# A hybrid decoder step on one core: in the first chunk, 24 GLU and merge tiles move into the attention stage

## The chip, the cores and the metric

The kernel runs on 1 core of one Trainium2 chip. The metric is the device time of one execution in microseconds (us); lower is better. The core has five engines that run side by side and meet at semaphores: TensorE (PE), VectorE (DVE), ScalarE (ACT), GpSimd (POOL) and SyncE (SP), which here only issues transfers. Sixteen DMA engines move the data.

## The reference, cut to what matters

One inference step of one layer over 1024 prompt tokens and 32 sample tokens, all in float32:

```
h = rmsnorm(x);  q, k, v, u, g_att, g_s5 = split(h @ w_in)
att = differential attention(q, k, v)          # 8 heads, causal, two softmaxes per head
s5y = diagonal complex SSM(u)                  # 64 groups x 64 states
z   = gelu(s5y)
s5o = z * sigmoid(z @ w_glu + b_glu)           # the GLU
merged = sigmoid(g_att) * (att @ w_proj_att) + sigmoid(g_s5) * (s5o @ w_proj_s5)
x = x + merged @ w_out
x = x + PEER(rmsnorm(x))                       # 8 heads, 16 gathered expert rows each
y = rmsnorm(x)
```

The GLU needs only z. The S5 half of `merged` needs s5o and h. The attention needs only q, k and v. The attention and the S5 half of `merged` therefore do not depend on each other.

## The kernel before, in words

**Front.** The norm, the projection of u and the whole SSM are computed for all tokens first. z is stored to DRAM; its first 256 columns also stay on chip (`AT_Z0`).

**Chunks and stages.** The rest runs over three chunks of token columns, `CHUNKS = ((0, 2), (2, 5), (5, 9))` in blocks of 128. A chunk passes through stages: `glu`, `s5` (the merge with the S5 gate), `v`, attention, `ga` (the merge with the attention gate), `out`, `query`. Each stage is a block with one in-order program per engine, and all engines meet at its end. The first chunk has 256 columns, and its values are computed earlier, so it has no `v` stage.

**Weight tiles.** GLU, merges, attention projections and queries use 128x1024 weight tiles of 512 KB, streamed through three buffers (`NWB = 3`) in the order of the list `stream`. SP issues the load of tile m once tile m-3 has been used (`load_tile`, L668). `stat_tile` (L674, matmuls on L678) multiplies one tile by the chunk's columns into one PSUM bank and raises `acc_ready`. In the first chunk before the attention there are 8 GLU tiles, 16 merge tiles (per output block a gate tile and a projection tile), and then, in the attention, 16 tiles: K and Q of 8 heads.

**GLU and merge.** For a GLU tile, ACT takes the sigmoid out of PSUM (L1301) and DVE multiplies it with z (L1309). For a merge pair, ACT takes the sigmoid of the gate tile (L1363) and DVE multiplies the projection tile with it (L1373).

**Attention, first chunk.** A unit is one head and one block of 128 queries; there are 8 heads with two units each. Order is written out by hand in `unit(n)` on each engine. Per head PE does: scores of the second unit (L1520, L1523), transposes of the first unit's probabilities (L1543), the K tile of the next head (L678), the value product (L1560), transposes of the second unit, the Q tile of the next head, the value product, K turned by token (L1502), and scores of the next head's first unit. DVE takes row maxima (L1684), forms the probabilities (L1691 to L1697) and copies K out of PSUM (L1672). ACT does the exponentials (L1602), copies probabilities, outputs, Q and K out of PSUM (L1634, L1610, L1587, L1593), and the roots of the per-head norm (L1621). Exponential, square root and sigmoid each need another activation table, and a change of function costs an ACT_TABLE_LOAD.

**Semaphores.** At the start of the first GLU stage SP waits for the last stores of the SSM and clears 60 spent semaphores (L1277), which later stages use again.

**Behind it.** From the first chunk's `query` stage on, POOL gathers expert rows for PEER, and every later stage carries a fixed plan of gather pairs (`PAIR_PLAN`). In the first chunk the plan is empty up to the query stage: `share(0, ...)` returns -2.

Of the kernel before, what the change touches and what calls it, by code (L numbers as in the profile page):

```python
# [56 lines left out]
def hybrid_step(nc, dr, out):  # L57

    root = ExitStack()
    with root:  # L60
        def sem(name):
            return root.enter_context(nc.semaphore(name))
# [1180 lines left out]
        def sem_again(name):  # L1243
# [3 lines left out]
        vslot, ko = lay(5120, [2, TT + 1, P]), lay(7424, [2, 4, P])  # L1247
        kslot, qslot = lay(21504, [2, T]), lay(21504 + 2 * T, [2, 416])
        causal = lay(24448, [P])
        nmax, coef, ssq = lay(24576, [2, 2]), lay(24580, [2, 1]), lay(24584, [2, 3])  # L1250
        junk_a, osb, lsum = lay(24592, [P]), lay(24720, [2, 3, P]), lay(25488, [4, 2])
        rsum = lay(25496, [4, 2])
        qs, ks = lay(25600, [H, NS]), lay(25856, [H, NS])
        names = ("at_in", "ko_ready", "ko_free", "s_ready", "m_ready", "e_ready", "l_ready", "p_ready",
                 "t_ready", "t_free", "o_ready", "o_free", "ss_ready", "rt_ready", "on_ready", "oT_ready", "oT_free",
                 "qs_ready", "part")
        (at_in, ko_ready, ko_free, s_ready, m_ready, e_ready, l_ready, p_ready, t_ready, t_free,
         o_ready, o_free, ss_ready, rt_ready, on_ready, oT_ready, oT_free, qs_ready, part) = (sem_again(n) for n in names)
        hist_in, vh_in, ko_out, k_out = ([sem_again(f"{n}{k}") for k in range(2)] for n in ("hist_in", "vh_in", "ko_out", "k_out"))
        n_units = 0  # L1260

        def stage_glu(c):
            lo, hi = chunk_cols(c)
            W, m0, fa0, gl0 = hi - lo, first_tile(c, "glu"), n_fa, c * KC
            zT = lay(AT_Z if c else AT_Z0, [KC, W])
            s5oT = lay(AT_S5O, [KC, W])
            with nc.Block(no_gpsimd_drain=True) as block:
                @block.sync
                def _(sp):
                    if c == 0:  # L1270
                        sp.wait_ge(sp_out, 16)
                        sp.wait_ge(ss_out, 16)
                        sp.wait_ge(zs_out, 16)
                        for k in range(2):
                            sp.wait_ge(z_out[k], 16 * (KC // 2))
                        for s in to_clear:
                            sp.sem_clear(s)  # L1277
                    for j in range(KC):
                        load_tile(sp, m0 + j + NWB)

                @block.tensor
                def _(pe):
                    if c:
                        pe.wait_ge(hz_in, 16 + 128 * c)
                    for j in range(KC):
                        if j >= 4:
                            pe.wait_ge(fa, fa0 + j - 3)
                        stat_tile(pe, m0 + j, j % 4, zT, W)
                        peer_pe(pe, share(c, "glu", j, KC))

                @block.scalar
                def _(act):
                    for j in range(KC):
                        peer_act(act, share(c, "glu", j, KC), behind=1)
                        if c == 0 and j == 0:
                            for k in range(2):
                                act.wait_ge(z_out[k], 16 * (KC // 2))
# [12 lines left out]

                @block.gpsimd
                def _(pool):
                    peer_pool(pool, share(c, "glu", 0, 1))


        def stage_merge(c, stage, fold):
# [5 lines left out]
            with nc.Block(no_gpsimd_drain=True) as block:  # L1322
                @block.sync
                def _(sp):
                    if not fold:
                        sp.dma_start(causal, dr["causal"]).then_inc(at_in, 16)
# [105 lines left out]
        def stage_attention(c):  # L1432
# [6 lines left out]
            stores = 2 if sampled else 1  # L1439
            N, early = H * nf, nf > 2  # L1440
            def turned(n):

                h = (n - 2) // nf - 1
                return h if (n - 2) % nf == 0 and 0 <= h < H else None
# [8 lines left out]
            with nc.Block(no_gpsimd_drain=True) as block:  # L1453
                @block.sync
                def _(sp):
# [7 lines left out]
                    def k_rows_out(h):  # L1463
# [13 lines left out]
                    for h in range(H):  # L1477
                        for j in (2 * h + 2, 2 * h + 3):
# [10 lines left out]
                def _(pe):  # L1489
                    def k_tile(h):  # L1490
                        if h:
                            pe.wait_ge(ko_free, h0_ + h)
                        stat_tile(pe, m0 + 2 * h, 7, hT, W)

                    def q_tile(h):
                        pe.wait_ge(fv, fv0 + h + 1)
                        stat_tile(pe, m0 + 2 * h + 1, 7, hT, W)

# [34 lines left out]
                    def unit(n):  # L1533
# [50 lines left out]
                def _(act):  # L1584
                    def q_in(h):
                        act.wait_ge(acc_ready, m0 + 2 * h + 2)
                        nc.scalar.activation(qslot[:, h % 2, 0:W], ps[:, 7, 0:W], ACT.Copy, scale=HD ** -0.5).then_inc(fa, 1)  # L1587
# [35 lines left out]
                    def outputs(h):  # L1623
                        act.wait_ge(oT_ready, h0_ + h + 1)
                        nc.scalar.activation(attT[:, h, 0:nf * P], ps[:, 6, 0:nf * P], ACT.Copy, scale=subln[:, 0:1]).then_inc(oT_free, 1)

                    def unit(n):
                        h, i = n // nf, n % nf
# [38 lines left out]
                def _(dve):  # L1667
                    def k_in(h):
                        dve.wait_ge(acc_ready, m0 + 2 * h + 1)
                        if h >= 2 and not sampled:  # L1670
# [34 lines left out]
                    def normalised(h):  # L1705
# [5 lines left out]
                                                ALU.mult).then_inc(on_ready, 1)  # L1711

                    def unit(n):
                        h, i = n // nf, n % nf
# [23 lines left out]
                    for n in range(N):  # L1738
                        unit(n)
                    for n in range(N, N + 3):  # L1740
                        if rooted(n) is not None:
# [487 lines left out]
        for c in range(len(CHUNKS)):  # L2229
            stage_glu(c)  # L2230
            n_fa += KC
            stage_merge(c, "s5", False)
            n_fa, n_fv = n_fa + KC, n_fv + KC
            if c:
                stage_values(c)
            stage_attention(c)
# [118 lines left out]
```

## Time and profile before

| what | value |
|---|---|
| three timed runs | 4268.94, 4269.66, 4274.7 us (median 4269.66) |
| the profiled execution | 4273.91 us, its span 4272.0 us |
| busy share of the span | PE 78%, DVE 70%, ACT 37%, POOL 31% |
| mean granted TensorE clock | 0.923 of full speed |
| gathered rows | 1056 issues of 128 rows, 65.9% of the 16 DMA engines' time |

The shares are means over stages with different limits. The stages that this change touches end at about 578 us of the span; before that POOL has next to nothing to do, and after about 700 us gathers keep the DMA engines busy nine tenths of the time. In the rows below, "idle before" is the time an engine stood still just before an instruction, and the name behind the arrow is what ended it; PEld is the weight load that runs beside the matmuls, and each tile shows as 16 matmuls of 128x256.

### The profile page before, as it was taken

To read this page: it belongs to the slowest core of one execution; us is meant where nothing else is said; L and a number is where in the kernel's file an instruction comes from. 1 tells how busy PE (TensorE), PEld (TensorE's weight loads), DVE (VectorE), ACT (ScalarE), POOL (GpSimd) and SP (SyncE) were. 2 spreads that over 40 slices of the span, in tenths; PEclk is the share of its full clock that TensorE was granted. 3 is DMA by queue.
4 is the path that set the end of the run, shared out by engine and by line. 5 is a ranking of instruction groups with operands and counts; after the bars stand their busy time and mean duration, and the time that the engine had idled before them with its cause. 6 is when DMAs were issued, how large, how long until landed. Compare 5 with 4: busy or idle time off the path is not lost. (4 is left out here: it accounts for less than half of the span.)

```text
span 4272.0 us, 43342 instructions
## 1 busy us (share of the span) xinstructions
PE 3319.6 (78%) x13280; PEld 1895.6 (44%) x13280; DVE 2972.3 (70%) x6144; ACT 1573.3 (37%) x4102; POOL 1305.2 (31%) x1145
## 2 busy tenths in 40 slices
PE   7989888787778688988677587967777777777776
PEld 5757776444544444455566443522222222222221
DVE  6483113788988888899666678976676766666664
ACT  2221321434753243477433233233333333333333
POOL 0100001332223333322332323644444444444443
PEclk9989999899989889989789788999999999999999
DMA  3023346998879999888899988999999999999997
GB/s 136 11 86 127 114 159 219 375 416 327 297 289 403 375 400 396 330 290 289 319 385 397 353 328 344 363 418 419 419 417 409 416 416 414 418 412 399 407 412 314
DMA packets 273722, 1411.58 MB, mean 330 GB/s; under 512 B 39090, under 2 KB 78482, under 8 KB 136402
## 3 DMA queue, kind: packets, MB, share of 16 engines
q0 software_dynamic: 158192, 1126.79, 65.9%
q1 hardware_dynamic: 114914, 281.88, 18.0%
q8 instruction: 106, 1.74, 0.2%
q14 instruction: 126, 1.03, 0.1%
q10 hardware_dynamic: 384, 0.13, 0.0%
HBM read 1367.90 MB, written 38.96 MB: 329 GB/s over the span
## 5 line engine op out<-in xcount | busy, mean ns | idle before, releaser
L953 POOL DMA_INDIRECT arena<-in_uv,arena x1056 | 1243.8, 1178 | 2227.4 <-DVE arena L1063 1328.0
L1053 DVE CUSTOM_DVE_ANT_0 arena<-arena 128x1024 f32<-128x1024 f32 x1056 | 1289.7, 1222 | 531.8 <-DMA arena<-in_uv,arena 504.0
L1193 PE MATMUL ps<-arena 128*128 128x512 f32 (+1 forms) x2288 | 1077.3, 615 | 407.5 <-ACT arena L1160 405.9
L678 PE MATMUL ps<-arena 128*128 128x256 f32 (+2 forms) x3456 | 1097.4, 478 | 125.8 <-DMA arena<-in_w_stat 54.5
L678 PEld LDWEIGHTS ps<-arena 128*128 128x128 f32 x3456 | 675.7, 198 | 510.4 <-issue 337.9
L1193 PEld LDWEIGHTS ps<-arena 128*128 128x128 f32 (+1 forms) x2288 | 410.0, 189 | 1074.1 <-ACT arena L1160 628.7
L1141 ACT ACTIVATE arena<-arena 128x2 f32<-128x2 f32 x528 | 107.2, 203 | 1475.9 <-DVE arena L1053 1444.3
L1063 DVE SCALAR_TENSOR_TENSOR arena<-arena 128x1024 f32<-128x1024 f32 x484 | 618.8, 1279 | 22.6 <-ACT arena L1150 22.5
L1150 ACT ACTIVATE arena<-arena 128x1 f32<-128x1 f32 x1056 | 253.4, 287 | 17.3
L1141 ACT ACT_TABLE_LOAD x168 | 215.5, 1283 | 46.2 <-PEq L1322 29.2
L1160 ACT ACTIVATE arena<-ident,arena 128x128 f32<-128x128 f32 x540 | 187.3, 394 | 8.8
L1862 PE MATMUL ps<-ident,arena 128*128 128x128 f32 x512 | 84.2, 315 | 86.1 <-DMA arena<-in_cache_k 62.4
L2064 PE MATMUL ps<-arena 128*128 128x512 f32 (+1 forms) x288 | 129.0, 609 | 26.8 <-PEq L1322 26.8
L1821 PE MATMUL ps<-arena 128*64 128x128 f32 x1024 | 142.6, 299 | 0.0
L1821 PEld LDWEIGHTS ps<-arena 128*64 128x64 f32 x1024 | 126.6, 152 | 13.0 <-issue 10.5
L307 PE MATMUL ps<-arena 128*128 128x512 f32 (+1 forms) x288 | 127.0, 603 | 3.8 <-PEq L118 3.8
L1684 DVE TENSOR_REDUCE arena<-ps 128x1 f32<-128x384 f32 (+5 forms) x128 | 90.7, 750 | 44.8 <-PE ps L1523 44.8
L959 POOL DMA_DIRECT2D arena<-in_iota x1 | 0.7, 718 | 378.7 <-POOLq L2020 378.7
L1406 PE MATMUL ps<-arena 128*128 128x512 f32 (+1 forms) x224 | 100.7, 612 | 17.7 <-PEq L1322 17.7
L1543 PE MATMUL ps<-ident,arena 128*128 128x128 f32 x288 | 50.1, 308 | 81.8 <-DVE arena L1697 81.7
L1862 PEld LDWEIGHTS ps<-ident,arena 128*128 128x128 f32 x512 | 65.1, 159 | 101.3 <-DMA arena<-in_cache_k 61.3
L1898 ACT ACTIVATE arena<-ps 128x512 f32<-128x512 f32 x128 | 69.5, 590 | 106.1 <-PE ps L1862 101.9
(255 smaller groups left out, 3321.2 us busy)
## 6 DMA issues: line engine op xcount, KB each, us to landing
arena<-in_w_stat SPq DMA_DIRECT2D x216, 512.0 KB
arena<-in_cache_k SPq DMA_DIRECT2D x64, 512.0 KB
arena<-in_cache_v SPq DMA_DIRECT2D x64, 512.0 KB
arena<-in_w_mov SPq DMA_DIRECT2D x14, 2048.0 KB, 12.5
arena<-in_uv,arena POOLq DMA_INDIRECT x1056
arena<-in_x SPq DMA_DIRECT2D x16, 512.0 KB, 9.5
arena<-scr_s POOLq DMA_DIRECT2D x40, 128.0 KB
scr_h<-arena SPq DMA_DIRECT2D x1, 4224.0 KB
```

The costliest lines, as they stand in the source:

```text
L307: last = nc.tensor.matmul(ps[0:rows, n % 4, :], tok, slab[:, k, kc, :], start=(kc == 0), stop=(kc == KC - 1))
L678: last = nc.tensor.matmul(ps[:, bank, 0:w], wbuf[m % NWB][:, kc * P:(kc + 1) * P], moving[:, kc, :], start=(kc == 0), stop=(kc == KC - 1))
L953: pool.indirect_dma_start(ring[s % RING], None, dr["uv"], bass.IndirectOffsetOnAxis(ap=idx[:, g % 4, j:j + 1], axis=0)).then_inc(row_in[s ...
L1053: nc.vector.tensor_tensor_reduce(ring[s % RING][:, 0:D], ring[s % RING][:, 0:D], h2r[:, b % 2, :], 1.0, 0.0, ALU.mult, ALU.add, act_in[:, ...
L1063: nc.vector.scalar_tensor_tensor(accr[:, b % 2, :], ring[s % RING][:, D:2 * D], wgt[:, s % RING:s % RING + 1], accr[:, b % 2, :], ALU.mult ...
L1141: nc.scalar.activation(act_out[:, p % 2, :], act_in[:, k:k + 2], ACT.Gelu).then_inc(gelu_d, 1)
L1150: last = nc.scalar.activation(wgt[:, k + q:k + q + 1], gates[:, g % 4, 2 * r + q:2 * r + q + 1], ACT.Copy, scale=act_out[:, p % 2, q:q + 1])
L1160: nc.scalar.activation(diag[:, n % 4, 0:m], pattern, ACT.Copy, scale=wgt[:, k + q:k + q + 1]).then_inc(diag_d, 1)
L1193: last = nc.tensor.matmul(ps[0:m, 4 * (b % 2) + c, :], diag[:, n % 4, 0:m], ring[s % RING][:, D + 512 * c:D + 512 * (c + 1)], start=start, ...
L1821: last = nc.tensor.matmul(flat_s[:, p * P:(p + 1) * P], qpad[:, h * ROWS:(h + 1) * ROWS], kT[:, n % 2, h, :], start=(h == 0), stop=(h == H ...
L1862: last = nc.tensor.transpose(ps[:, t % 3, j * P:(j + 1) * P], kpg[:, n % NKB, h * P:(h + 1) * P], ident[:, :])
L2064: last = nc.tensor.matmul(ps[0:rows, 2 * (b % 2) + k, :], mT[:, kc, (b - b0) * P:(b - b0) * P + rows], o_slab[:, k, kc, :], start=(kc == 0 ...
```

## The change

The stages `glu` and `s5` of the first chunk are gone as stages. Their 24 tiles ("side tiles", numbered e = 0 to 23: 8 GLU tiles, then 8 pairs of gate and projection) are dealt to the 16 attention units: one before PE's wait for each unit's probabilities and a third at each head's end. The side tiles use PSUM banks 1, 3 and 5. Their sigmoids and products get places in ACT's and DVE's unit order; a projection tile has no sigmoid and a gate tile no product of its own. The weight stream of the chunk is reordered to match. For the first chunk the attention's small buffers move to another part of on-chip memory, the attention gets fresh semaphores, and SP's waits and clears move behind the first head's stores. Chunks 1 and 2 are unchanged.

```diff
+        def first_kq(h, k):
+            return 1 - k if h == 0 else 5 * h - (2 if k else 0)
+        def first_side(e):
+            return 5 * (e // 3) + 2 + (e % 3 if e // 3 == H - 1 else 2 * (e % 3))
+        for h in range(H):
+            for k in range(2):
+                stream[first_kq(h, k)] = T_QK + 2 * h + k
+        for e in range(3 * KC):
+            stream[first_side(e)] = T_GLU + e if e < KC else T_GS + e - KC
...
+        AT_FREE = 27268
+        side_s5, side_g = lay(AT_FREE, [KC, 2 * P]), lay(AT_FREE + 2 * D, [2, 2 * P])
+        AT_SMALL = (AT_FREE + 3 * D, 21504, 21504)
...
@@ stage_attention, SP @@
+                    if c == 0:
+                        sp.dma_start(causal, dr["causal"]).then_inc(at_in, 16)
                     head_in(0)
                     head_in(1)
+                    for m in range(2 if c == 0 else 0):
+                        load_tile(sp, m + NWB)
                     k_rows_out(0)
+                    if c == 0:
+                        sp.wait_ge(sp_out, 16)
...
+                        for s in to_clear:
+                            sp.sem_clear(s)
+                        for h in range(H):
+                            if 0 < h < H - 1:
+                                sp.wait_ge(o_ready, h * nf)
+                                sp.wait_ge(k_out[(h - 1) % 2], 16 * ((h - 1) // 2 + 1))
+                                head_in(h + 1)
+                            for j in range(4 if h < H - 1 else 3):
+                                load_tile(sp, 5 * h + 2 + j + NWB)
+                            if h < H - 1:
+                                k_rows_out(h + 1)
+                                load_tile(sp, 5 * h + 6 + NWB)
@@ stage_attention, PE @@
+                    def side_tile(e):
+                        g, half = side_of(e)
+                        if e >= 3:
+                            old, half_old = side_of(e - 3)
+                            if half_old:
+                                pe.wait_ge(side_merged, old - KC + 1)
+                            else:
+                                pe.wait_ge(side_gate, old + 1)
+                        if half and g == KC:
+                            pe.wait_ge(gl_used, KC)
+                        moving = zT if half is None else side_s5 if half else hT
+                        stat_tile(pe, first_side(e), (1, 3, 5)[e % 3], moving, W)
...
                             scores((n + 1) // nf, (n + 1) % nf)
+                        if c == 0:
+                            side_tile(3 * h + i)
                         pe.wait_ge(p_ready, u + 1)
...
                                 scores(h + 1, 0)
+                        if c == 0 and crossing:
+                            side_tile(3 * h + 2)
...
+                    if c == 0:
+                        pe.wait_ge(hz_in, 16)
                     pe.wait_ge(at_in, 16 * (c + 1))
@@ stage_attention, ACT, unit(n) @@
                             q_in(h + 1)
+                        if c == 0:
+                            for e in (3 * h - 1, 3 * h) if i == 0 else (3 * h + 1,):
+                                if e >= 0:
+                                    side_sigmoid(e)
@@ stage_attention, DVE, unit(n) @@
                             maxima((n + 1) // nf, (n + 1) % nf)
+                        if c == 0 and i == 0 and h:
+                            side_product(3 * h - 2)
+                            side_product(3 * h - 1)
...
+                        if c == 0 and crossing:
+                            side_product(3 * h)
@@ main loop @@
-            stage_glu(c)
-            n_fa += KC
-            stage_merge(c, "s5", False)
             if c:
+                stage_glu(c)
+                n_fa += KC
+                stage_merge(c, "s5", False)
```

What the order of the instructions becomes is shown at three places. First PE in the middle of a head. In the program before, L1520 and L1523 are scores, L1543 and L1530 transposes, L678 with x8 one tile, L1560 the value product and L1502 K by token:

```order
L1523 MATMUL ps<-arena,ident 128x128 x2
L1520 MATMUL ps<-arena 128x256 x2
L1523 MATMUL ps<-arena,ident 128x128 x2
L1543 MATMUL ps<-ident,arena 128x128
L1530 MATMUL ps<-ident,arena 128x128 x2
L678 MATMUL ps<-arena 128x256 x8
L1560 MATMUL ps<-arena 128x128
L1543 MATMUL ps<-ident,arena 128x128 x2
L678 MATMUL ps<-arena 128x256 x8
L1560 MATMUL ps<-arena 128x128 x2
```

In the changed program the same instructions stand on L1571 and L1574 (scores), L1596 and L1581 (transposes), L692 (tiles) and L1613 (value product):

```order
L1574 MATMUL ps<-arena,ident 128x128 x2
L692 MATMUL ps<-arena 128x256 x8
L1571 MATMUL ps<-arena 128x256 x2
L1574 MATMUL ps<-arena,ident 128x128 x2
L692 MATMUL ps<-arena 128x256 x8
L1596 MATMUL ps<-ident,arena 128x128
L1581 MATMUL ps<-ident,arena 128x128 x2
L692 MATMUL ps<-arena 128x256 x8
L1613 MATMUL ps<-arena 128x128
L692 MATMUL ps<-arena 128x256 x8
L1596 MATMUL ps<-ident,arena 128x128 x2
L692 MATMUL ps<-arena 128x256 x8
```

Two of a head's five tiles are the K and Q tiles as before; the other three stand ahead of the second scores, ahead of the first transposes and ahead of the second transposes.

Second ACT from a head's first output copy to the next head's first exponentials. Before, L1610 is the output copy, L1634 the probability copy, L1617 the squares, L1621 the roots, L1587 and L1593 the copies of Q and K, L1602 the exponentials:

```order
L1610 ACTIVATE arena<-ps,arena 128x128
L1634 ACTIVATE arena<-ps 128x256
L1617 ACTIVATE arena<-arena 128x128
L1621 ACT_TABLE_LOAD
L1621 ACTIVATE arena<-arena 128x2
L1587 ACTIVATE arena<-ps 128x256
L1593 ACTIVATE arena<-ps 128x256
L1602 ACT_TABLE_LOAD
L1602 ACTIVATE arena<-ps,arena 128x128 x2
```

In the changed program, with the same operations on L1667, L1704, L1674, L1678, L1644, L1650 and L1659, and a side tile's sigmoid on L1695:

```order
L1667 ACTIVATE arena<-ps,arena 128x128
L1704 ACTIVATE arena<-ps 128x256
L1674 ACTIVATE arena<-arena 128x128
L1678 ACT_TABLE_LOAD
L1678 ACTIVATE arena<-arena 128x2
L1644 ACTIVATE arena<-ps 128x256
L1695 ACT_TABLE_LOAD
L1695 ACTIVATE arena<-ps 128x256
L1650 ACTIVATE arena<-ps 128x256
L1659 ACT_TABLE_LOAD
L1659 ACTIVATE arena<-ps,arena 128x128 x2
```

A sigmoid with a table of its own now stands between the copies of Q and K, ahead of the exponentials.

Third SP at the start. Before, it clears the semaphores (ISA, L1277), loads 8 GLU tiles, the causal mask and 16 merge tiles, and then the attention's values (out_v) and K rows:

```order
L1277 ISA x60
L672 DMA arena<-in_w_stat 128x1024 x8
L1267 UNCONDITIONAL_BRANCH
L1323 UNCONDITIONAL_BRANCH
L1326 DMA arena<-in_causal 128x128
L672 DMA arena<-in_w_stat 128x1024 x16
```

Now:

```order
L1489 DMA arena<-in_causal 128x128
L1475 DMA arena<-out_v 128x2x128 x2
L686 DMA arena<-in_w_stat 128x1024 x2
L1481 DMA out_k<-arena 128x2x128
L1486 DMA scr_k<-arena 128x256
L1504 ISA x60
L686 DMA arena<-in_w_stat 128x1024 x4
L1481 DMA out_k<-arena 128x2x128
```

The mask is now the first transfer of the stage whose first matmul waits for it, and the clears stand behind the first K rows and ahead of the sixth tile's load.

## Rows read from the trace of the kernel before

**Rows 1.** Stretches: busy PE, PEld, DVE, ACT, POOL; then granted clock, DMA share, GB/s

```profile
367.83:398.76 30.93, 29.42 (x128) 25.34 (x129) 3.40 (x8) 5.08 (x9) 0.00 (x0) 0.95 0.47 144
398.76:455.33 56.57, 55.49 (x257) 48.57 (x257) 3.40 (x8) 3.07 (x8) 0.00 (x0) 1.00 0.49 150
455.33:578.03 122.70, 95.43 (x489) 76.31 (x489) 31.00 (x112) 58.15 (x175) 0.00 (x0) 0.94 0.31 99
720.00:4272.00 3552.00, 2693.27 (x9817) 1421.35 (x9815) 2660.66 (x5438) 1393.43 (x3537) 1282.76 (x1125) 0.92 0.94 374
```

**Rows 2.** Timeline of the merge: two gate sigmoids, two tiles apart

```profile
402.49 0.38 ACT L1363 ACTIVATE arena<-ps 128x256 f32<-128x256 f32 x1 [4.73 <-PE ps L678]
409.40 0.38 ACT L1363 ACTIVATE arena<-ps 128x256 f32<-128x256 f32 x1 [6.52 <-PE ps L678]
```

**Rows 3.** Timeline of one head of the attention, all engines

```profile
509.19 0.70 PE L1520 MATMUL ps<-arena 64*128 64x256 f32 x4 [1.53 <-ACT arena L1602]
510.37 0.27 PE L1543 MATMUL ps<-ident,arena 128*128 128x128 f32 x1
510.70 3.62 PE L678 MATMUL ps<-arena 128*128 128x256 f32 x16
514.15 0.39 PE L1560 MATMUL ps<-arena 128*128 128x128 f32 x2
514.36 0.42 DVE L1672 COPY arena<-ps 128x256 f32<-128x256 f32 x1 [3.03 <-PE ps L678]
515.68 0.44 PE L1543 MATMUL ps<-ident,arena 128*128 128x128 f32 x2 [1.14 <-DVE arena L1697]
515.96 3.62 PE L678 MATMUL ps<-arena 128*128 128x256 f32 x16
519.41 0.61 PE L1560 MATMUL ps<-arena 128*128 128x128 f32 x4
519.61 0.38 ACT L1587 ACTIVATE arena<-ps 128x256 f32<-128x256 f32 x1 [1.27 <-PE ps L678]
520.52 0.38 ACT L1593 ACTIVATE arena<-ps 128x256 f32<-128x256 f32 x1 [0.53 <-PE ps L1502]
520.93 1.28 ACT L1602 ACT_TABLE_LOAD   x1
522.22 0.37 ACT L1602 ACTIVATE arena<-ps,arena 128x128 f32<-128x128 f32 x1
523.08 0.70 PE L1520 MATMUL ps<-arena 64*128 64x256 f32 x4 [1.53 <-ACT arena L1602]
```

**Rows 4.** Start of the GLU stage: SP and PE, then one slice as in rows 1

```profile
362.12 0.57 SPq L688 DMA_DIRECT2D arena<-scr_h  x1
364.84 2.54 SPq L715 DMA_DIRECT2D scr_z<-arena  x2
367.83 29.43 PE L678 MATMUL ps<-arena 128*128 128x256 f32 x128 [2.59 <-PEq L698]
...
369.00:370.00 1.00, 1.00 (x4) 0.82 (x3) 0.00 (x0) 0.00 (x0) 0.00 (x0) 0.50 0.55 221
```

**Rows 5.** Line L715, the stores of z

```profile
DMA to landing us min/median/max: 2.6/2.7/4.4
```

**Rows 6.** Groups of ACT, 367 to 578 us: busy us, mean ns, idle before

```profile
L1602 ACT ACT_TABLE_LOAD x7 | 9.0, 1283 | 0.1
L1621 ACT ACT_TABLE_LOAD x7 | 9.0, 1283 | 0.1
L1301 ACT ACTIVATE arena<-ps,b_glu 128x256 f32<-128x256 f32 x8 | 3.8, 474 | 19.5 <-PE ps L678 19.5
```

**Rows 7.** Timeline of PE: the seventh head, and the last one's beginning

```profile
550.86 0.70 PE L1520 MATMUL ps<-arena 64*128 64x256 f32 x4 [1.53 <-ACT arena L1602]
552.82 4.85 PE L678 MATMUL ps<-arena 128*128 128x256 f32 x16
566.44 0.70 PE L1520 MATMUL ps<-arena 64*128 64x256 f32 x4 [1.53 <-ACT arena L1602]
```

More of the change, by code:

```diff
@@ L1247, in hybrid_step, with att_small @@
         vslot, ko = lay(5120, [2, TT + 1, P]), lay(7424, [2, 4, P])
[L1248 to L1252, printed above, removed]
+        def att_small(at):
+            return (lay(at, [2, T]), lay(at + 2 * T, [2, 416]), lay(at + 2944, [P]), lay(at + 3072, [2, 2]), lay(at + 3076, [2, 1]),
+                    lay(at + 3080, [2, 3]), lay(at + 3088, [P]), lay(at + 3216, [2, 3, P]), lay(at + 3984, [4, 2]), lay(at + 3992, [4, 2]))
+        AT_FREE = 27268
+        side_s5, side_g = lay(AT_FREE, [KC, 2 * P]), lay(AT_FREE + 2 * D, [2, 2 * P])
+        AT_SMALL = (AT_FREE + 3 * D, 21504, 21504)
         qs, ks = lay(25600, [H, NS]), lay(25856, [H, NS])
+        kslot, qslot = att_small(AT_SMALL[-1])[0:2]
         names = ("at_in", "ko_ready", "ko_free", "s_ready", "m_ready", "e_ready", "l_ready", "p_ready",
@@ L1257, in hybrid_step @@
         (at_in, ko_ready, ko_free, s_ready, m_ready, e_ready, l_ready, p_ready, t_ready, t_free,
-         o_ready, o_free, ss_ready, rt_ready, on_ready, oT_ready, oT_free, qs_ready, part) = (sem_again(n) for n in names)
-        hist_in, vh_in, ko_out, k_out = ([sem_again(f"{n}{k}") for k in range(2)] for n in ("hist_in", "vh_in", "ko_out", "k_out"))
+         o_ready, o_free, ss_ready, rt_ready, on_ready, oT_ready, oT_free, qs_ready, part) = (sem(n) for n in names)
+        side_gate, side_merged = sem("side_gate"), sem("side_merged")
+        hist_in, vh_in, ko_out, k_out = ([sem(f"{n}{k}") for k in range(2)] for n in ("hist_in", "vh_in", "ko_out", "k_out"))
         n_units = 0
@@ L1269, in _ @@
                 def _(sp):
[L1270 to L1277, printed above, removed]
                     for j in range(KC):
@@ L1294, in _ @@
                         peer_act(act, share(c, "glu", j, KC), behind=1)
-                        if c == 0 and j == 0:
-                            for k in range(2):
-                                act.wait_ge(z_out[k], 16 * (KC // 2))
                         act.wait_ge(acc_ready, m0 + j + 1)
@@ L1440, in stage_attention, with kq_tile, side_of @@
             N, early = H * nf, nf > 2
+            kslot, qslot, causal, nmax, coef, ssq, junk_a, osb, lsum, rsum = att_small(AT_SMALL[c])
+            zT, mT = lay(AT_Z0, [KC, W]), lay(AT_MT, [KC, W])
+            def kq_tile(h, k):
+                return m0 + 2 * h + 1 - k if c else first_kq(h, k)
+            def side_of(e):
+                return (e, None) if e < KC else (KC + (e - KC) // 2, (e - KC) % 2)
             def turned(n):
@@ L1475, in _ @@
                     head_in(1)
+                    for m in range(2 if c == 0 else 0):
+                        load_tile(sp, m + NWB)
                     k_rows_out(0)
-                    for h in range(H):
+                    if c == 0:
+                        sp.wait_ge(sp_out, 16)
+                        sp.wait_ge(ss_out, 16)
+                        sp.wait_ge(zs_out, 16)
+                        for k in range(2):
+                            sp.wait_ge(z_out[k], 16 * (KC // 2))
+                        for s in to_clear:
[10 more added lines that the diff above has]
+                                load_tile(sp, 5 * h + 6 + NWB)
+                    for h in range(H if c else 0):
                         for j in (2 * h + 2, 2 * h + 3):
@@ L1625, in outputs, with side_sigmoid @@
                         nc.scalar.activation(attT[:, h, 0:nf * P], ps[:, 6, 0:nf * P], ACT.Copy, scale=subln[:, 0:1]).then_inc(oT_free, 1)
+                    def side_sigmoid(e):
+                        g, half = side_of(e)
+                        if half:
+                            return
+                        act.wait_ge(acc_ready, first_side(e) + 1)
+                        if g >= 2:
+                            if g - 2 < KC:
+                                act.wait_ge(gl_used, g - 1)
+                            else:
+                                act.wait_ge(side_merged, g - 1 - KC)
+                        bias = {} if e >= KC else {"bias": b_glu[:, e:e + 1]}
+                        nc.scalar.activation(side_g[:, g % 2, :], ps[:, (1, 3, 5)[e % 3], 0:W], ACT.Sigmoid, **bias).then_inc(side_gate, 1)
                     def unit(n):
@@ L1711, in normalised, with side_product @@
                                                 ALU.mult).then_inc(on_ready, 1)
+                    def side_product(e):
+                        g, half = side_of(e)
+                        if half == 0:
+                            return
+                        dve.wait_ge(side_gate, g + 1)
+                        if half is None:
+                            nc.vector.tensor_tensor(side_s5[:, g, :], zT[:, g, :], side_g[:, g % 2, :], ALU.mult).then_inc(gl_used, 1)
+                        else:
+                            dve.wait_ge(acc_ready, first_side(e) + 1)
+                            nc.vector.tensor_tensor(mT[:, g - KC, :], ps[:, (1, 3, 5)[e % 3], 0:W], side_g[:, g % 2, :],
+                                                    ALU.mult).then_inc(side_merged, 1)
                     def unit(n):
@@ L1739, in _ @@
                         unit(n)
+                    for e in (3 * H - 2, 3 * H - 1) if c == 0 else ():
+                        side_product(e)
                     for n in range(N, N + 3):
```

17 lines of the change are left out of this document (8 added, 9 removed).

## The prediction

> **What bounds the kernel now.** I read the stretches by stage first [rows 1]. In the GLU and merge stages PE is busy 29.42 of 30.93 us and 55.49 of 56.57 us: PE alone sets their length, and ACT and DVE work about 3 to 5 us in each. In the attention stage PE is busy only 95.43 of 122.70 us, so about 27 us of it are waits, and ACT works 58.15 us there. None of the three stages carries gathers. Everything behind them, the gathers with their DMA share of 0.94 included, starts when they have ended, so what they lose or gain should move the end by the same amount.
>
> Then I read the timeline of one head [rows 3]. PE's second scores start at 509.19 and the next head's at 523.08: 13.89 us per head. PE stands still twice. It waits 1.53 us before the second scores, because ACT must copy Q and K, load the exponential table and do the first exponentials (519.61 to about 523.0) before the score banks are free. It waits 1.14 us before the second transposes, because DVE's K copy (514.36), queued ahead of the probabilities, waits for the K tile. Both are latencies of a chain, not a lack of throughput.
>
> **The change part by part.** All sums are made against the profiled execution: 4273.91 us, span 4272.0.
>
> *Removed:* the two stages, 367.83 to 455.33 [rows 1]: -87.5 us, with their launch gaps and the GLU's slow first tiles.
>
> *Added to PE:* 24 tiles. Two tiles lie 6.91 us apart in the merge (402.49 to 409.40, [rows 2]), so a tile costs 3.455 us and 24 cost +82.9.
>
> *The waits the tiles cover.* I walk one middle head with T = 0 at its second scores, with the steps of [rows 3]: scores until 1.18, side tile A until 4.64, transposes, K tile 4.97 to 8.42, value product 0.39, side tile B until 12.27, second transposes 0.28, Q tile until 16.00, then value product, K by token and first scores (13.89 - 1.53 - 10.22 = 2.14) until 18.14, side tile C until 21.60, next second scores. Without a wait that is 13.89 + 10.37 - 2.67 = 21.59. A tile shows 3.62 but the next instruction starts 3.45 later; this overlap of 0.17 now also holds at the two places where a wait stood, so I take 21.25: 3.0 saved per head (2.67 at least). From head 0's second scores to head 7's there are seven such steps: -21.0 (bounds -18.7 and -21.0).
>
> *Are the chains now in time?* First the exponentials. Q's copy starts 0.20 after its tile; before, the second scores could go 3.67 after the tile's end (519.41 to 523.08). The new sigmoid between the copies costs a table load of 1.28 and 0.47 [rows 6], of which 0.53 fills ACT's idle time before the K copy (520.52, [rows 3]): release at 3.67 + 1.75 - 0.53 = 4.9. PE arrives at 2.14 + 3.46 = 5.6, or 5.3 with the overlap. It fits by 0.4 to 0.7 us: the tightest place. Second the probabilities. ACT's whole attention work is 58.15 / 8 = 7.3 us per head [rows 1], of which about 2.2 are table loads [rows 6]; the half after the first transposes is some 2.5 to 3. So its sigmoids end at about 4.64 + 3 + 1.28 + 0.95 = 9.9. DVE then does a product and the K copy (0.42 each; the product has its shape) and needs 0.9 more (515.68 - 514.78): 11.6, against PE's arrival at 12.27. It fits by 0.6. Per head ACT gets to about 10.5 of 21 us: the 7.3, 14 more loads (14 x 1.28 / 8 = 2.2) and 16 sigmoids (0.9).
>
> *Weight loads.* A merge tile's load is issued when the tile three before it is done, which leaves two tiles, 6.9 us, and PE does not wait for it in the merge [rows 1]. In the new order K and score work lies between, so the lead is 7.7 us or more, and I cost the loads at nothing. This needs SP on time: it now stands in front of them with K row stores, which wait for ACT's K copy, with value loads, and once with the 60 clears. The clears run while head 0's chain and tile 2 hold PE; without that cover they would be late once by a few us.
>
> *The last head.* It has no K and Q tiles. Before it takes 566.44 to 578.03, 11.59 us [rows 1, 7]. The tiles there cover the probability wait and some of ACT's work behind the last value product, but one more root table load (1.28) comes on the path, because sigmoids now stand between the roots. I take -2.4 (bounds 0 and -4).
>
> *The start.* The attention's first matmul now waits for the mask, whose load SP can issue only at the stage's start, about 367.9, behind the z stores (364.84 and after); DMA is still at 221 GB/s at 369 to 370 [rows 4]. No row shows the mask alone. Stores of z take 2.6 to 4.4 us to land, 2.7 in the median [rows 5]. Before, PE started at 367.83. So +2.7; from below 0, since hT's load (362.12) is early enough, from above 4.6.
>
> *TensorE's clock.* The GLU's first tiles ran at a granted clock of 0.50, the 1.2 GHz level, after PE had stood 2.59 us [rows 4], and that slowness went with the removed stage: 29.43 us against 8 x 3.455 = 27.6. The first K tile now starts after a longer stop: +1.6 (0 to 3.5, a whole tile at half rate). In the seventh head the tile at 552.82 took 4.85 and the head 566.44 - 550.86 = 15.58 [rows 7], 1.7 more than usual, after the 1.53 wait. With PE closed up I take that as gone: -1.7 (0 to -1.7).
>
> *One new wait.* The first projection tile (e = 9) needs all 8 GLU products. The last stands on DVE behind the row maxima of the second scores, while PE is at the tile right after these scores. Maxima of a size like the K copy's, twice, and a product of 0.42 give +1.5 once (0 to 2.2).
>
> Sum: -87.5 + 82.9 - 21.0 - 2.4 + 2.7 + 1.6 - 1.7 + 1.5 = -23.9. That is 4250.0 for the profiled execution. The median of the runs shown, 4269.66, is 4.25 below that execution, so I forecast 4246 us.
>
> **A rule that speaks against the change.** In the trace a change of function costs ACT 1.28 us and nothing around it: the load at 520.93 starts 0.03 after the K copy's end and the exponential starts at 522.22, right behind it [rows 3]. Now there are 29 loads (8 exponential, 8 root, 13 sigmoid, counted in the program) for 15 before. The Trainium skill, page "ScalarE: Activation LUTs", section "What ACT_TABLE_LOAD costs", puts a switch at about 1283 ns plus a drain of about 1380 ns, 2.66 us, and its section on table sets asks to batch calls by set. By its drain the two switches in front of the exponentials would cost 2.8 us more and PE would wait some 2 us at each of five head ends, some 10 us in all. The trace shows the load's length as the page has it, and no drain.
>
> **The rivals.**
>
> *ACT's switches bind.* If a switch costs twice its row, 1.28 more, the exponentials are released at 4.9 + 2.56 = 7.5 against PE's 5.6: 1.9 us of new wait at the five head ends that have a sigmoid there (h = 0, 1, 2, 3, 5), +9.6: 4256. For it: the margin there is only 0.4 to 0.7. Against it: no gap in [rows 3]. The page named above states such a price.
>
> *Given back behind 720 us.* The later stages hold 2693 us of PE work at a granted clock of 0.92 [rows 1]. A clock lower by 0.005 would cost at most 0.005 x 2693 / 0.92 = 15 us: 4246 + 15 = 4261. Nothing in these stages changes but their start, so the sign is open; the three runs lie 5.8 us apart.
>
> *Slower: the loads' queue closes a ring.* SP's load of the next head's tile B stands behind the K row stores, which wait for ACT's K copy, which now stands behind a sigmoid, which waits for PE. In the walk the K copy ends at 16.0 + 0.20 + 0.38 + 1.75 + 0.38 = 18.7, the load is released by PE at 21.6, and its tile is used 8.8 us later, 1.9 more than the 6.9 that do in the merge. PE waits once ACT is later than 2.9 + 1.9 = 4.8 us. The gain is gone when each of seven heads loses 3.4 us, with ACT 8.2 late, and at 11 us late the kernel is 7 x 6.2 - 23.9 = 19.5 slower: 4289. Only several long stops on ACT per head could do this; it is half busy.
>
> *The tiles cover nothing.* If the chains simply shift behind the tiles, only launch gaps and start terms are left: -87.5 + 82.9 + 2.7 + 1.6 + 1.5 = +1.2, 4271, no change. Against it: both waits start before the tile's place in PE's order, not behind it.
>
> **How the numbers follow.** Forecast 0.80, with its own terms at their bounds from 4238 to 4257; ACT's switches 0.06; given back 0.06; tiles cover nothing 0.03; the ring 0.05. A measurement of this kernel can tell about 0.2%, 8.5 us, from no change. Faster by more, below 4261: the forecast, the switches and half of what is given back, 0.88. Within 0.2%: 0.07. Slower: 0.05. The range of 8 in 10 runs from 4238, the lower bounds together, to 4261.
>
> **What would show it.** Right: a stage from about 368 to 553 in place of 367.83 to 578.03, 21.3 us from second scores to second scores, PE busy over 93% in it, no wait before second scores and second transposes. Start: the first tile at 370 to 371. The new wait: one stop of about 1.5 us ahead of tile 9 in the fourth head. Wrong: heads above 23 us with PE released by the exponentials (switches) or by in_w_stat (ring), or a stage that is short as said while the stretch behind it is longer than 3694 us, the 4272.0 - 578.0 of before.

## The result, and the profile after

In the first comparison the kernel after took 4238.25 us (median of 4 runs, 4232.8 to 4251.76), the kernel before 4272.18 (4 runs, 4268.94 to 4275.98): a ratio of 0.9929, with a 95% interval of 0.9909 to 0.9949. Timed again (e1, 5 runs), it took 4247.22 against 4270.76: 0.9951, 0.9939 to 0.9964. The two intervals overlap from 0.9939 to 0.9949, some 22 to 26 us. The forecast was 4246, a gain of 23.9, with a range of 4238 to 4261. The first median stands at the very lower end of that range, the second next to the forecast.

The profiled execution of after took 4251.76 us, span 4250.0, the longest of its four. Its stage in the form of [rows 1] (span of the stretch, busy PE, PEld, DVE, ACT, POOL, then granted clock, DMA share, GB/s), and what lies behind it:

```profile
372.54:563.04 190.50, 175.41 (x873) 146.90 (x873) 38.37 (x131) 83.17 (x206) 0.00 (x0) 0.97 0.44 137
...
563.04:4250.00 3686.96, 2823.03 (x10352) 1519.89 (x10352) 2686.70 (x5503) 1407.89 (x3566) 1289.26 (x1137) 0.92 0.93 368
```

One stage of 190.50 us stands where three stood, counted from the end of the last turn of z (PE's last transposes of z, with which the front ends). In before that end is at 365.24 and the next stage starts at 578.03: 212.79. So the stage gave 22.3 us. The span is 22.0 shorter, but not by the stage alone: the front, whose code is the same, ended 7.3 us later (372.54 for 365.24), and the stretch behind the stage was 7.0 shorter (3686.96 for 3693.97). These two are taken up under e1 and e8.

One head in the steady stretch, PE and then ACT, beside [rows 3] (start, duration, engine, line, operation; the bracket is idle time and its releaser):

```profile
501.33 0.70 PE L1571 MATMUL ps<-arena 64*128 64x256 f32 x4
...
502.51 3.62 PE L692 MATMUL ps<-arena 128*128 128x256 f32 x16
...
509.97 3.62 PE L692 MATMUL ps<-arena 128*128 128x256 f32 x16
513.43 0.38 PE L1596 MATMUL ps<-ident,arena 128*128 128x128 f32 x2
513.65 3.62 PE L692 MATMUL ps<-arena 128*128 128x256 f32 x16
517.10 0.61 PE L1613 MATMUL ps<-arena 128*128 128x128 f32 x4
...
519.08 3.62 PE L692 MATMUL ps<-arena 128*128 128x256 f32 x16
522.63 0.70 PE L1571 MATMUL ps<-arena 64*128 64x256 f32 x4
```

```profile
517.30 0.38 ACT L1644 ACTIVATE arena<-ps 128x256 f32<-128x256 f32 x1 [1.27 <-PE ps L692]
517.71 1.28 ACT L1695 ACT_TABLE_LOAD   x1
519.00 0.38 ACT L1695 ACTIVATE arena<-ps 128x256 f32<-128x256 f32 x1
519.28 0.38 ACT L1650 ACTIVATE arena<-ps 128x256 f32<-128x256 f32 x1
519.67 1.28 ACT L1659 ACT_TABLE_LOAD   x1
...
521.58 0.20 ACT L1659 ACTIVATION_READ_ACCUMULATOR arena<-ps,arena 128x1 f32 x1
```

No PE row has a bracket: the side tiles A, B and C (502.51, 509.97, 519.08) lie in the places that the prediction walks through, and neither the second transposes (513.43) nor the second scores (522.63) wait. The head takes 21.30 us. ACT's rows are the tightest place: behind the Q copy come a table load, the sigmoid, the K copy, the exponentials' load. The scores' banks are free at about 521.78, the end of the last row, 4.67 after the Q tile's end (517.1, where the next instruction starts); PE comes 5.52 after it. That leaves 0.85 us.

Where PE does stand in this stage, and its clock by head:

```profile
378.59 5.82 PE L692 MATMUL ps<-arena 128*128 128x256 f32 x16 [6.05 <-DMA arena<-in_causal]
...
392.15 0.70 PE L1571 MATMUL ps<-arena 64*128 64x256 f32 x4 [1.53 <-ACT arena L1659]
...
459.85 3.69 PE L692 MATMUL ps<-arena 128*128 128x256 f32 x16 [1.22 <-issue]
...
561.60 0.41 PE L1581 MATMUL ps<-ident,arena 128*128 128x128 f32 x2 [2.84 <-DVE arena L1784]
```

```profile
392.15:414.91 22.76, 22.73 (x108) 19.03 (x108) 4.23 (x15) 7.46 (x20) 0.00 (x0) 0.93 0.34 111
414.91:435.98 21.07, 21.04 (x108) 17.79 (x107) 4.76 (x17) 10.88 (x26) 0.00 (x0) 1.00 0.44 144
...
457.28:480.04 22.76, 21.50 (x111) 18.09 (x110) 4.58 (x17) 10.75 (x26) 0.00 (x0) 1.00 0.43 133
...
522.63:543.92 21.29, 21.26 (x110) 18.01 (x109) 4.17 (x15) 9.20 (x24) 0.00 (x0) 1.00 0.47 142
```

The first head is slow by its clock (0.93), the fourth by the stop ahead of tile 9, the others take 21.07 to 21.30. The mask load that the start waits for, answering to [rows 4, 5], and ACT's table loads, answering to [rows 6]:

```profile
372.14 2.54 SPq L729 DMA_DIRECT2D scr_z<-arena  x2
375.08 0.33 SPq L1489 DMA_DIRECT2D arena<-in_causal  x1
```

```profile
DMA to landing us min/median/max: 3.4/3.4/3.4
```

```profile
L1695 ACT ACT_TABLE_LOAD x13 | 16.7, 1283 | 0.2
...
L1659 ACT ACT_TABLE_LOAD x8 | 10.3, 1283 | 0.1
L1678 ACT ACT_TABLE_LOAD x8 | 10.3, 1283 | 0.1
```

These are 29 loads, as counted in the prediction, with 0.4 us of idle time ahead of them in all.

### The profile page after: what moved, and what is told of

The parts are those of the page before. It is cut to its first block and busy times, and to the rows that moved or that the text cites. A ratio compares the mean times of both kernels' runs of the same rounds, so it can differ in the third digit from the quotient of the medians.

```text
span 4250.0 us, 43333 instructions
## 1 busy us (share of the span) xinstructions
PE 3320.8 (78%) x13280; PEld 1894.4 (45%) x13280; DVE 2971.2 (70%) x6144; ACT 1589.8 (37%) x4116; POOL 1304.1 (31%) x1145
## 5 line engine op out<-in xcount | busy, mean ns | idle before, releaser
L692 PE MATMUL ps<-arena 128*128 128x256 f32 (+2 forms) x3456 | 1104.0, 479 | 129.8 <-DMA arena<-in_w_stat 52.5
L692 PEld LDWEIGHTS ps<-arena 128*128 128x128 f32 x3456 | 675.0, 199 | 514.7 <-issue 338.0
L1955 PE MATMUL ps<-ident,arena 128*128 128x128 f32 x512 | 81.9, 309 | 83.7 <-DMA arena<-in_cache_k 60.5
L1704 ACT ACTIVATE arena<-ps 128x128 f32<-128x128 f32 (+6 forms) x64 | 41.5, 649 | 173.6 <-PE ps L1596 173.4
```

Source lines behind the costliest of these rows:

```text
L692: last = nc.tensor.matmul(ps[:, bank, 0:w], wbuf[m % NWB][:, kc * P:(kc + 1) * P], moving[:, kc, :], start=(kc == 0), stop=(kc == KC - 1))
L1955: last = nc.tensor.transpose(ps[:, t % 3, j * P:(j + 1) * P], kpg[:, n % NKB, h * P:(h + 1) * P], ident[:, :])
```

## The experiments

Eight experiments ran, e1 to e4 in one session and e5 to e8 in another, on another chip. "Stage" in the table means: from the end of the last turn of z to the next stage's first tile, in one profiled execution. Ratios are to the kernel before, timed on the same chip; stages of e2 to e7 are compared with that of e1.

| run | ratio (95%) | stage us | behind it us |
|---|---|---|---|
| before, first profile | | 212.79 | 3694.0 |
| after, first profile | 0.9929 (0.9909 to 0.9949) | 190.50 | 3687.0 |
| e1 after again | 0.9951 (0.9939 to 0.9964) | 189.75 | 3687.7 |
| e2 undealt | 0.9990 (0.9978 to 1.0001) | 213.23 | 3685.5 |
| e3 early mask | 0.9953 (0.9940 to 0.9966) | 186.76 | 3685.3 |
| e4 four edits | 0.9935 (0.9922 to 0.9948) | 182.30 | 3690.9 |
| e5 tile C moved | 1.0011 (0.9998 to 1.0024) | 216.87 | 3686.9 |
| e6 tile B moved | 0.9980 (0.9967 to 0.9994) | 203.64 | 3683.3 |
| e7 more switches | 0.9977 (0.9966 to 0.9988) | 203.83 | 3697.3 |
| e8 before again | 0.9997 (0.9982 to 1.0012) | 212.75 | 3689.8 |

**e1 and e8: the two kernels again**, unchanged.

> The changed kernel, unchanged, timed again in five rounds and profiled again. The first profiles give a stage that is 22.3 us shorter (190.5 for 212.8), a front of identical code that ran 7.3 us longer and a stretch behind the stage that ran 7.0 us shorter; the timed medians differ by 33.9. Theory A (the stage is the only cause, the rest is the scatter of the clock): the stage is again 189 to 192 us, heads 21.1 to 21.3, the front is back near 365 us and the stretch behind it between 3680 and 3694; timed difference from before 22 to 34 us. Theory B (the work behind the stage has become faster because of the change): the stretch behind the stage is again 3687 us or less, while the front goes back to 365, and the timed difference is again above 30 us.

> The kernel before, unchanged, profiled and timed again: how much the same instructions scatter. The stage boundaries 367.83 to 578.03 are expected within 4 us of their places by the front's clock, the three stages again 212 to 214 us from the last turn of z to the next stage, the seventh head again 15.6 us, and the stretch behind between 3680 and 3695 us. Theory A (the difference of the kernels is the stage's 22 to 24 us): this stretch overlaps with the 3685 to 3691 us of the changed kernels. Theory B (the change also shortens what lies behind): it stays at 3694 or above.

The stages repeat within 0.8 us, 189.75 and 190.50 against 212.75 and 212.79: 22.3 to 23.0 us. The front of after ended at 364.37 this time, and that of before at 363.95: the 7.3 us were not of the change. The stretch behind is 3687.0 and 3687.7 for after, 3689.8 and 3694.0 for before; e4 and e7, which have the new stage too, stand at 3690.9 and 3697.3, so it overlaps. The timed gain of e1 is 23.5. Nothing here asks for a gain behind the stage, though a small one, below the scatter, is not excluded.

**e2: one stage, nothing dealt.** The 24 tiles stand at the stage's start:

```
-    if c == 0:
-        side_tile(3 * h + i)
...
-    if c == 0 and crossing:
-        side_tile(3 * h + 2)
...
     if c == 0:
         pe.wait_ge(hz_in, 16)
+        for e in range(3 * KC):
+            side_tile(e)
```

(the sigmoids, products and weight loads go to the start with them, and the values' loads and the first K row stores move behind the semaphore clears).

> One stage as in the changed kernel, but its 24 tiles stand back to back at its start, ahead of the first K tile, and not among the attention's units. Theory A (the gain comes from tiles that cover the waits inside the heads, 7 x 3.0 us and 2.4 in the last): the waits of 1.53 and 1.14 us per head are back, heads are 13.9 us, the stage is 83 us of tiles and 124 us of attention, 207 to 213 us in all, and the kernel is 16 to 24 us slower than the changed one, 0 to 8 us faster than before. Theory B (the gain comes from two stage boundaries less, their launch gaps and slow first tiles): stage near 191 us, time within 5 us of the changed kernel.

```profile
510.20 0.70 PE L1562 MATMUL ps<-arena 64*128 64x256 f32 x4 [1.53 <-ACT arena L1648]
516.69 0.44 PE L1585 MATMUL ps<-ident,arena 128*128 128x128 f32 x2 [1.14 <-DVE arena L1758]
...
524.10 0.70 PE L1562 MATMUL ps<-arena 64*128 64x256 f32 x4 [1.53 <-ACT arena L1648]
```

Both waits are back, and a head takes 13.90. From the last turn of z to the first Q tile it is 91.51 us for 94.30 of before: joining the stages saves 2.8, about the two launch gaps of before (1.51 and 1.07). But the first two heads take 16.45 and 15.30 for 14.87 and 13.67, at a granted clock of 0.81 and 0.89 for 0.89 and 1.00, which gives 3.2 back, and the stage is as long as the three were (213.23 for 212.75). So of the 23 us the dealing gives 20 at least. The median, 6.7 us below that of before with an interval on the ratio that holds 1, is within theory A's 0 to 8.

**e3: the mask a block earlier.**

```
     load_hT(sp, 0)
+    sp.dma_start(lay(AT_MASK0, [P]), dr["causal"]).then_inc(at_in, 16)
```

> The changed kernel with the load of the causal mask issued one block earlier, right behind the load of hT. Theory A (the first K tile waits for this load alone): the wait of 6.05 us ahead of the first K tile falls to about 2.6, as before the change, and the slow first tile (5.82 us) may fall to some 4: 3.5 to 5.5 us faster than the changed kernel. Theory B (the wait is the launch of the stage or the values' stores): the wait stays above 5 us, no change.

```profile
370.97 6.54 PE L692 MATMUL ps<-arena 128*128 128x256 f32 x16 [3.28 <-DMA arena<-in_causal]
```

```profile
365.18 0.66 SPq L734 DMA_DIRECT2D arena<-in_causal  x1
```

The wait falls from 5.85 to 3.28, not to 2.6: the load goes out 2.5 us ahead of the last turn's end and no longer 2.5 behind it, but takes 5.7 us to land (3.4 in after), beside hT's load and the z stores. And the first tile gets longer, 6.54 for 5.32 of e1, because it runs at a granted clock of 0.50 to about 376.7, nearly to its end. From the end of the last turn to the second scores it is 17.55 for 18.92, 1.4 us better. Head 0 gains another 1.6 by its clock, although the wait ahead of it is the same:

```profile
385.24 0.70 PE L1571 MATMUL ps<-arena 64*128 64x256 f32 x4 [1.53 <-ACT arena L1659]
386.43 3.62 PE L692 MATMUL ps<-arena 128*128 128x256 f32 x16
```

The stage is 3.0 shorter, where 3.5 to 5.5 were expected. The time does not show that (0.9953 for 0.9951), and could not, with intervals of 0.13%.

**e4: the mask, and the three other stops.**

```
+    if c == 0 and n == 0:
+        side_tile(0)                          # PE: ahead of scores(0, 1)
     scores((n + 1) // nf, (n + 1) % nf)
...
+    if c == 0 and i == 0 and h == 3:
+        side_product(3 * h - 2)               # DVE: ahead of the maxima
     maxima((n + 1) // nf, (n + 1) % nf)
...
+    if c == 0 and n == N - 1:
+        side_sigmoid(3 * h + 1)               # ACT: ahead of the last roots
     if rooted(n) is not None:
         roots(rooted(n))
```

> The changed kernel with four edits: the mask load a block earlier; in head 3 the eighth GLU product ahead of the row maxima; the first projection tile ahead of the scores of the first unit's successor; the last sigmoid ahead of the last roots. Theory A (each remaining stop is the latency that it was read as): start 3.5 to 5.5 us shorter, the stop of 1.22 us ahead of tile 9 gone, the stop of 1.53 us in the first head gone, the tail 0 to 1.4 us shorter: 6 to 10 us faster than the changed kernel, stage near 182 us. Theory B (the stops move on to the next instruction in line): under 3 us beyond what the early mask alone gives.

```profile
443.55 0.70 PE L1571 MATMUL ps<-arena 64*128 64x256 f32 x4
...
444.73 3.62 PE L692 MATMUL ps<-arena 128*128 128x256 f32 x16
...
545.00 0.41 PE L1581 MATMUL ps<-ident,arena 128*128 128x128 f32 x2 [1.44 <-DVE arena L1788]
```

Tile 9 (444.73) does not wait, the 1.53 of the first head is gone, and the tail's 2.84 is 1.44. The stage is 182.30, 7.5 below e1, and the median 8.1 below: the stops were what they were read as, and none moved on. It has the lowest median of its session, but at 0.9935 against 0.9951 the two intervals overlap, so the times alone do not separate it from e1.

**e5 and e6: one tile out of its place.** In e5 tile C goes beside tile B, in e6 tile B beside tile A (the order of the weight loads follows, not shown):

```
     if c == 0:
         side_tile(3 * h + i)
+        if i:
+            side_tile(3 * h + 2)              # e5
-    if c == 0 and crossing:
-        side_tile(3 * h + 2)
...
-        side_tile(3 * h + i)
+        for e in (3 * h, 3 * h + 1) if i == 0 else ():
+            side_tile(e)                      # e6
```

> The changed kernel, but the third tile of each head (C) stands beside the second one (B), ahead of the second transposes; nothing stands ahead of the next head's second scores. Theory A (tile C covers the exponentials' chain): in the changed kernel the exponentials are done 4.67 us after the Q tile and PE comes after 5.52; without tile C it comes after 2.06, so it waits 2.6 us at the five head ends that have a sigmoid and about 1.5 at the other two: 16 us slower than the changed kernel. Theory B (the tiles' place does not matter, PE is simply full): within 4 us of the changed kernel.

> The changed kernel, but the second tile of each head (B) stands beside the first one (A), ahead of the first transposes; nothing stands between the value product behind the K tile and the second transposes. Theory A (tile B covers DVE's K copy and the probabilities behind it): the wait of 1.14 us ahead of the second transposes is back, up to 2.2 where ACT's sigmoids hold DVE's products up: 8 to 15 us slower than the changed kernel. Theory B (place does not matter): within 4 us.

```profile
411.72 1.23 PE L1571 MATMUL ps<-arena 64*128 64x256 f32 x4 [1.53 <-ACT arena L1659]
437.14 0.70 PE L1571 MATMUL ps<-arena 64*128 64x256 f32 x4 [2.67 <-ACT arena L1659]
...
539.66 0.70 PE L1571 MATMUL ps<-arena 64*128 64x256 f32 x4 [2.59 <-ACT arena L1659]
```

```profile
411.72:437.14 25.42, 22.71 (x108) 19.06 (x108) 4.86 (x18) 10.89 (x27) 0.00 (x0) 0.93 0.38 120
437.14:461.18 24.04, 21.33 (x110) 18.17 (x110) 4.85 (x18) 11.19 (x28) 0.00 (x0) 1.00 0.41 126
461.18:489.54 28.36, 24.51 (x109) 20.29 (x109) 4.51 (x17) 10.75 (x27) 0.00 (x0) 0.88 0.35 107
```

```profile
412.00:413.00 1.00, 1.00 (x5) 0.35 (x5) 0.48 (x2) 0.00 (x0) 0.00 (x0) 0.50 0.81 246
```

In e5 the seven waits come as worked out from ACT's rows, 1.53 to 2.68, 15.1 us in all for 16 expected (the first is 1.53 for 2.6). But the stage is 27.1 longer than e1's. Of these, 3.7 lie in the last head and 23.4 in the seven steps before it, 8.3 more than the waits: in four of the seven steps, beyond the slow first head that e1 has too, the clock falls to 0.50, the lower level of 1.2 GHz, behind a wait, as at 412 us, and the mean goes to 0.93 or 0.88. The step from 437.14, whose clock stays at 1.00, is 24.04: a head of 21.3 and its wait. So the places of the tiles matter, and the waits of e5 cost more than themselves. In e6 the waits ahead of the second transposes are back at 1.14 to 1.52, 8.5 us; the clock of the heads behind the first stays at 1.00 up to the last, so there a wait costs its length and the lost overlap of 0.2. With 3.9 more in the last head (clock 0.93) the stage is 13.9 longer, inside the 8 to 15 of theory A.

**e7: two more switches per head end.**

```
+    nc.scalar.activation(extra[:, 2 * h:2 * h + 1], ident[:, 0:1], ACT.Sqrt)
+    nc.scalar.activation(extra[:, 2 * h + 1:2 * h + 2], ident[:, 0:1], ACT.Sigmoid)
```

> The changed kernel with two more tiny activations (a square root and a sigmoid of one column, results unused) on ACT at each of the seven head ends, ahead of the K copy, so that two more table loads stand in front of the exponentials: 2 x (1.28 + 0.21) = 3.0 us. Theory A (a switch costs its table load and nothing else; the slack in front of the second scores is 5.52 - 4.67 = 0.85): PE waits 3.0 - 0.85 = 2.1 us at five head ends and some 0.5 at two, 12 us slower than the changed kernel. Theory B (the Trainium skill, page ScalarE: Activation LUTs, section What ACT_TABLE_LOAD costs, adds a drain of about 1380 ns to a switch): 2.8 us more per head end, about 31 us slower. Theory C (the changed kernel was already bound there): all 3.0 us at seven places, 21 us slower.

```profile
524.45 1.28 ACT L1722 ACT_TABLE_LOAD   x1
525.74 0.20 ACT L1722 ACTIVATE arena<-ident 128x1 f32<-128x1 f32 x1
525.95 1.28 ACT L1723 ACT_TABLE_LOAD   x1
527.24 0.20 ACT L1723 ACTIVATE arena<-ident 128x1 f32<-128x1 f32 x1
527.35 0.36 ACT L1651 ACTIVATE arena<-ps 128x256 f32<-128x256 f32 x1
527.73 1.28 ACT L1660 ACT_TABLE_LOAD   x1
```

```profile
529.89 0.70 PE L1572 MATMUL ps<-arena 64*128 64x256 f32 x4 [2.15 <-ACT arena L1660]
```

A switch takes 1.5 with its activation, back to back: no drain. PE waits 2.15 to 2.24 at four of the five head ends with a sigmoid: that is 3.0 less the slack of 0.85. It waits 0.82 at the first and not at all at the two without (0.5 expected), 9.6 us in all for 12. The first is shorter because its sigmoid finds its table still in place and needs no load (the Q copy, then the sigmoid):

```profile
402.70 0.38 ACT L1645 ACTIVATE arena<-ps 128x256 f32<-128x256 f32 x1 [2.78 <-PE ps L692]
402.98 0.47 ACT L1696 ACTIVATE arena<-ps,b_glu 128x256 f32<-128x256 f32 x1
```

Theory A holds for the waits. Another 4.5 us came mostly from the clock again (0.93 and 0.88 in two heads), so that the stage is 14.1 longer. The 31 of the drain and the 21 of a bound kernel are excluded.

## Why the prediction was right

By its own steps, against the two profiles of after (first, again):

| part | before | forecast | after | again |
|---|---|---|---|---|
| last turn of z to first K tile | 90.09 | 5.3 | 6.05 | 5.85 |
| first K tile to second scores | 11.43 | 13.0 | 13.56 | 13.07 |
| seven heads, 21 side tiles | 99.68 | 151.0 | 151.77 | 151.72 |
| last head, 3 side tiles | 11.59 | 19.6 | 19.12 | 19.11 |
| sum | 212.79 | 188.9 | 190.50 | 189.75 |

*Tiles and covered waits:* right. A middle head came to 21.07 to 21.30 for 21.25, so a wait of 1.53 and one of 1.14 went, and 0.3 by the overlap. The second transposes do not wait, as worked out (a margin of 0.6). That the tiles' places do it, and not the fewer stages, was argued and is now shown (e2, e5, e6). The rival by which the tiles cover nothing would have given e2's time.

*The tightest place:* released at 4.67 for 4.9, PE there at 5.52 for 5.3 to 5.6; margin 0.85 for 0.4 to 0.7. The slack is some 0.2 larger than I had said at best, and e7 shows the price beyond it. The rival by which ACT's switches bind would have shown waits at five head ends; there are none. It counted one end too many: the first head's sigmoid needs no load, as seen in e7.

*The start:* +3.5 for +2.7. The mask was issued 2.54 after the end of the z turn, as the rows of SP said, but landed 3.4 later; the z stores' 2.7 that I took from [rows 5] was too low, their 4.4 too high.

*The clock:* +1.6 was too low in the first profile and about right in the second: the first K tile, 3.69 in before, took 5.82 and 5.32, so 2.1 and 1.6 more. The first head took 22.76 and 22.70, 1.4 to 1.5 above the others: behind its wait of 1.53 the clock fell, and side tile 0 took 5.1 and 4.7 us for 3.6. The prediction has no term for that. It came out near all the same, because the first head of before was slow in the same way, 14.87 for 13.89 (first row below), and so 1.0 of it stood in the sum without being named. The wait alone does not do it: in e3 the same wait left the clock at full, and why is open. On the other side, the slow seventh head (0.89 in before, 15.58 us, 15.57 in e2 and again in e8) is gone as forecast.

*The last head:* it gained 2.8 for 2.4, but mostly by something that the term did not name. Its clock, 0.61 before, is 1.00: PE's busy time without the three tiles fell from 5.5 to 3.7 us, which is 1.8. Its waits fell only by 1.0, from 5.1 to 4.1. The coverage that I had priced at 2.4 was too high, and the sum came near by luck:

```profile
466.76:481.63 14.87, 12.48 (x59) 10.02 (x59) 3.18 (x12) 3.94 (x16) 0.00 (x0) 0.89 0.26 93
...
550.86:566.44 15.58, 12.87 (x62) 10.51 (x62) 3.86 (x15) 7.61 (x23) 0.00 (x0) 0.89 0.32 102
566.44:578.03 11.59, 5.46 (x24) 3.24 (x24) 3.77 (x14) 6.35 (x22) 0.00 (x0) 0.61 0.25 88
```

*Tile 9:* 1.22 us for 1.5, in the fourth head; e4 removes it by the one product that it was said to be.

*Weight loads and the ring:* no side tile waits for its load in either profile.

*PE's share:* over 93 was named for a stage counted, like 367.83, from 2.59 us behind the last turn of z. Counted so, PE is busy 175.41 of 187.91 us, 93%, as said; of the whole 190.50 it is 92%. The "368 to 553" of the prediction is 185 us, but its own sum gives 186.3; 187.9 and 187.2 (again) were measured.

*Given back behind the stage:* not seen. What remains open is the scatter: the stretch of same code behind the stage was between 3683 and 3697 us over ten profiles, and the front ended between 364 and 373. That this scatter made the 34 us of the first timing, where the stage gives 22 to 23, is likely but not shown, since its three faster executions have no profile. The second timing's 4247 is what the stage explains; that the first one's 4238 still lay within the range is luck.

## What to carry to other kernels

A wait for a chain on other engines is worth as much as independent work that can be put in front of the waiting instruction: list the waits of one period, walk the period with the new pieces in place, and check that each chain ends before PE gets there. Joining stages is the means, not the gain. When a short wait of TensorE goes, look at the granted clock behind it as well. One that is left or added can cost more than its length: 15.1 us of waits cost 23.4 in e5, while in e6 the 8.5 us cost 10.1.

## What the runs showed of the hardware

- Behind a stop of 1.5 to 2.7 us TensorE's granted clock sometimes fell to 0.50, mostly for some 3 us, and sometimes not: in e5, 2.67 us at 437.14 left the head at 1.00, while 1.53 us at 411.72 took it to 0.93. Behind two stops in a row (2.68 and 1.23) at 461 to 464 it stood at 0.50 for over 6 us, and a tile took 6.64. Ahead of the first head the same 1.53 took the next tile to 4.6 to 5.1 us in after, e1, e5 and e7, and left it at 3.62 in e3. In one place it repeated: 15.58, 15.57 and 15.57 us for the seventh head in two profiles of before and one of e2.
- A shorter stop need not give a warmer start: after 5.85 us of waiting (e1) the first tile took 5.32, after 3.28 (e3) it took 6.54. The tile started at 370.22 and had full clock from 374 us in the one, at 370.97 and from some 377 in the other.
- A transfer issued earlier took longer: the same mask load landed 3.4 us after its issue behind the z stores and 5.7 when issued 5 us sooner among them; of those 5 us, 2.6 came through.
- Two table switches with tiny activations in a row ran in 2.90 us without a gap (524.45 to 527.35 in e7). The Trainium skill, page "ScalarE: Activation LUTs", section "What ACT_TABLE_LOAD costs", adds a drain of about 1380 ns to a switch; no run here shows it.
